# The second mixer of a two-block transformer on one core, put in another order: stick breaking by pairs of heads, output products moved up, values projected as features

## Chip, cores and metric

One NeuronCore of one Trainium2 chip runs the whole program in one launch. The metric is device time in microseconds, the median of three runs.

## What is computed

The input is 256 tokens of width 1024. A first block (two layers of half-step gated feed-forward, attention and gated feed-forward) comes before the part that is changed and is the same in both kernels. The second block begins with the mixer of the reference, cut here to its core:

```
proj = rms_norm(x) @ w_in        # q_a 512, k_a 128, v_a 128, q_b 512, k_b 512, v_b 512, gates 2 x 1024
y_a  = window attention with sinks (8 query heads, 2 key heads of 64), q and k normed per head
y_b  = stick breaking (8 heads): z = q k / 8; log_keep = log_sigmoid(-z) before the diagonal, else 0
       suffix = reversed cumsum(log_keep) - log_keep
       weights = exp(log_sigmoid(z) + suffix) before the diagonal, else 0;  y_b = weights @ v_b
x = x + (sigmoid(gate_a) * (y_a @ w_up_swa) + sigmoid(gate_b) * (y_b @ w_up_sb)) @ w_out
```

After it comes a feed-forward layer with experts picked by product keys: 16 query units, a choice of 16 rows for each of 8 heads, and 256 gathers of 1 MB (128 rows of two vectors of 1024 numbers).

## The kernel before

**Layout.** Activations stand transposed, as eight tiles of 128 features by 256 tokens. Each matrix is cut into units of 128 x 1024 numbers that stream from HBM into a ring of nine raw buffers. To reach the accuracy of float32, each unit is split in two: ScalarE copies it rounded into `WH` (`hi`, line 639), VectorE subtracts to get `WL` (`lo`, line 969), and each product is three matmuls (lines 535 to 537: high by high, high by low, low by high). WH and WL are rings of five units. A call of `hi` or `lo` for a unit also does the three units after it, as far as the ring is free, and a unit's slot comes free when TensorE has used the unit five places back. A product of one unit with 256 tokens is 24 matmuls of 256 columns.

**Order.** No scheduler orders the work: each engine has its own hand-written program (`pe_program`, `act_program`, `dve_program`, `pool_program`, `sp_program`), runs it strictly in order, and waits on semaphores that count the other engines' steps. A waiting instruction holds up everything behind it on its engine.

**Opening of the mixer.** TensorE makes the four `qa` units and `ka`; VectorE scales each out of PSUM (line 1301). In the pass for `ka` it first multiplies the residual `hT` by the last norm's gains, eight instructions (line 1297), so that this stands ahead of the output of `ka`. ScalarE squares the five results (822), TensorE sums the squares (1877), ScalarE takes roots (824, 826), VectorE reciprocals and the norm (`qk_norm`, 1307 and 1309). `va` is made with tokens as rows: 48 matmuls of 128 columns (1887 to 1889). `vb` is 48 matmuls of 512 columns (1900 to 1902) into banks 2 and 3, and waits for the roots, which are read out of these banks. VectorE scales them (1319, 1327).

**Window attention.** Seven turns of a loop over four pairs of heads (scores, exponent, transposes, values). In each turn a *fill* stands behind the scores: two units of `qb`, `kb` or the gates `gt`, 48 matmuls into bank 7, put out by VectorE (`rest`, line 1343) at the end of its own turn. Fill n waits until the output of fill n-1 is out.

**Stick breaking.** Two halves of four heads, one after the other. Each half: logits (1966, 1967), copy out of PSUM (1381), min(-z, z) (1383), on ScalarE exp (871) and ln(1 + .) (873), two fills, softplus (1386) and two masks, suffix sums by triangular matmuls (1974 to 1976), subtraction (1394), clip (1396), exp (877), two masks (1399, 1400), values (1994, 1995), output split in YH and YL (691, 1035). The first half has one fill more, ahead of its values. With each fill VectorE makes two WL units and then later puts the fill out. In all 5 fills.

**End of the mixer.** ScalarE takes the 16 sigmoids (886). Eight `upab` units follow, each with its left half multiplied with the window branch (YH, YL 0 to 3) and its right half with the stick-breaking branch (4 to 7), 12 matmuls each, through banks 6, 7, 0, 1. VectorE multiplies by the gates (1416), GpSimd adds (609), ScalarE and VectorE split the sum (890, 1408). Then eight `wout` units (192 matmuls, 1025 for their output), which wait for those splits tile by tile, and the query units `pq`.

Of the kernel before, what the change touches and what calls it, by code (L numbers as in the profile page):

```python
# [9 lines left out]
ALU = mybir.AluOpType  # L10
# [4 lines left out]
T = 256  # L15
# [241 lines left out]
def program(nc, wst, cst, x, skt, uv, out, vscr, units):  # L257
    ctx = ExitStack()
    with ctx:
# [95 lines left out]
        Z = flat(AST)[:, 0:1536]  # L355
        W = flat(APT)
        E1 = view(s2, 1536)
        E2 = A[:, used[s2]:used[s2] + 1536]
        assert used[s2] + 1536 <= ARENA
# [66 lines left out]
        s_snk, s_snke = sem("sink_shifted"), sem("sink_exp")  # L426
        s_z, s_zc, s_e1, s_e1l, s_sm, s_cum, s_sbw, s_wm, s_we, s_wk, s_sbp = (sem(n) for n in (
# [198 lines left out]
        def act_program(ac):  # L626
# [196 lines left out]
            ac.wait_ge(s_qas, 1)  # L823
            ac.activation(RS[:, 0:4, :], PS[:, 2:4, :].rearrange("p a (b t) -> p (a b) t", b=2), ACT.Sqrt,
                          bias=c("eps", 1, 2), scale=1.0).then_inc(s_qrs, 1)
            ac.activation(RS[:, 4, :], PS[:, 4, 0:T], ACT.Sqrt, bias=c("eps", 0, 1), scale=1.0 / 64).then_inc(s_qrs, 1)
# [18 lines left out]
            n = 4  # L845
# [23 lines left out]
            for half in range(2):  # L869
                ac.wait_ge(s_e1, half + 1)  # L870
                own(ac.activation(E1, E1, ACT.Exp))
                own.wait()
                ac.activation(E1, E1, ACT.Ln, bias=c("eps", 2, 3)).then_inc(s_e1l, 1)
                fill()
                fill()
                ac.wait_ge(s_wm, half + 1)
                ac.activation(W, W, ACT.Exp).then_inc(s_we, 1)
                if fills[0] < len(FILL):
                    fill()
                for t in (2 * half, 2 * half + 1):  # L880
                    ac.wait_ge(s_sbp, t + 1)
                    copy_out(YH, 4 + t, 6 + t % 2, O_SB + t)
            for t in range(8):
# [74 lines left out]
        def dve_program(dv):  # L958
# [322 lines left out]
            for t in range(5):  # L1281
# [13 lines left out]
                if t == 4:  # L1295
                    for kc in range(8):
                        ins = dv.scalar_tensor_tensor(out=hT[:, kc, :], in0=hT[:, kc, :], scalar=c("gains", 48 + kc, 49 + kc),
                                                      in1=RT[:, 0, :], op0=ALU.mult, op1=ALU.mult)
                    ins.then_inc(s_hf, 1)
# [11 lines left out]

            dv.wait_ge(s_qrs, 2)
            qk_norm(4)
            qk_norm(0)
            lo("va", 0)
            dv.wait_ge(s_used, U("va", 0))
            dv.wait_ge(s_rtk, 2)
            for blk in range(2):
                ins = dv.tensor_scalar(VA[:, blk, :], PS[:, 1, 128 * blk:128 * blk + 128], RTK[:, blk:blk + 1], None, ALU.mult)
            ins.then_inc(s_va, 1)  # L1320
            for t in (1, 2, 3):
                qk_norm(t)
            for t in range(4):
                lo("vb", t)
            dv.wait_ge(s_used, U("vb", 3))
            for blk in range(2):
                ins = dv.tensor_scalar(VB[:, blk, :], PS[:, 2 + blk, :], RTK[:, blk:blk + 1], None, ALU.mult)
            ins.then_inc(s_vb, 1)

            fills = [0]  # L1330

            def fill():
# [6 lines left out]
                lo(name, t + 1)  # L1339

# [32 lines left out]
            def h4(v):  # L1373
                return v.rearrange("p (h k) -> p h k", h=4)

            Zh, Sh, Wh = h4(Z), h4(E2), h4(W)
            mk = c("sbmask").unsqueeze(1).broadcast_to([128, 4, 128])
            for half in range(2):
# [11 lines left out]
                for rest in filled:  # L1390
                    rest()
# [741 lines left out]
```

## Time and profile before

| what | value |
|---|---|
| median of three runs | 2043.84 us (2041.53 to 2045.69) |
| the profiled execution | 2047.32 us, its span 2045.4 us |
| TensorE busy | 1863.1 us, 91% |
| VectorE, ScalarE, GpSimd busy | 1303.7 (64%), 907.0 (44%), 305.9 us (15%) |
| mean granted TensorE clock | 0.969 |
| the mixer's stretch that the diff touches | about 1152 to 1361.5 us of the span |
| gathers of the last layer | from 1379 us to the end, 407 to 410 GB/s |

Of a timeline row the first number is the start and the second the time from there to the end of the row's last instruction; "x4" are four instructions together; in brackets stands how long the engine was idle before it and who released it. Matmuls overlap, so their pitch is read from starts and not from durations. A granted clock of 1.00 is 2.4 GHz and 0.50 is 1.2 GHz.

### The profile page before, as it was taken

Reading aid. Unit: us, or ns where it says so; the run is one execution under the profiler, and the core shown is the slowest. Engines: PE = TensorE matmul, PEld = TensorE weight load, DVE = VectorE, ACT = ScalarE, POOL = GpSimd, SP = SyncE. Lnnn points to the kernel's source line nnn. Section 1 sums busy time; section 2 is a strip of 40 time slices with the busy share of each in tenths; the row PEclk is TensorE's granted clock in tenths of the full one; section 3 lists DMA queues with packets and bytes.
Section 4 is the critical chain, followed back from the end, with each engine's and each line's share of the span. In section 5 each row is a group of like instructions: output and inputs, shape, how many; then the busy total and the mean of one; then the engine's idle time right before and its main releaser. Section 6 shows DMA issues by size and latency. Waiting matters only on the chain.

```text
span 2045.4 us, 29867 instructions
## 1 busy us (share of the span) xinstructions
PE 1863.1 (91%) x11568; PEld 1495.6 (73%) x11568; DVE 1303.7 (64%) x2378; ACT 907.0 (44%) x1865; POOL 305.9 (15%) x340
## 2 busy tenths in 40 slices
PE   7999999999999999999999988899997877778877
PEld 7999889999999999869999878797533322223222
DVE  5555785655655562686555765577587767676454
ACT  4444464444444441474444443543454443444333
POOL 1000101000100010000000100023343333333331
PEclk9999899999999997899999899899999999999999
DMA  7555426955555534205555243249999999999998
GB/s 274 186 186 178 128 77 141 305 186 186 161 186 187 185 114 166 83 22 166 186 186 186 83 144 104 83 165 375 387 422 421 421 422 422 421 421 421 422 421 323
DMA packets 96972, 488.35 MB, mean 239 GB/s; under 512 B 10640, under 2 KB 10896, under 8 KB 63808
## 3 DMA queue, kind: packets, MB, share of 16 engines
q0 software_dynamic: 38368, 274.74, 34.9%
q1 hardware_dynamic: 58464, 211.70, 30.9%
q8 instruction: 92, 1.51, 0.3%
q14 instruction: 48, 0.39, 0.1%
HBM read 482.21 MB, written 4.19 MB: 238 GB/s over the span
## 4 chain that ended last, share of the span: by engine, by line
PE 61%; DMA 12%; DVE 11%; issue 8%; POOL 4%; ACT 3%; another core or an unknown queue 0%; POOLq 0%; ACTq 0%; SPq 0%; DVEq 0%
PE PS L535 16%; PE PS L536 15%; PE PS L537 15%; PE PS L2025 3%; DMA WH<-uv,A 3%; DMA YL<-uv,A 3%; DMA YH<-uv,A 2%; DMA raw<-uv,A 2%; DVE WL L969 2%; PE PS L2046 2%; PE PS L1540 1%; DMA A<-uv,A 1%; DMA WL<-uv,A 1%; DVE XL L977 1%; DMA XF<-uv,A 1%
## 5 line engine op out<-in xcount | busy, mean ns | idle before, releaser
L969 DVE TENSOR_TENSOR WL<-raw,WH 128x1024 fp32r<-128x1024 f32 (+1 forms) x379 | 451.7, 1234 | 92.4 <-ACT WH L639 91.8
L535 PE MATMUL PS<-XH,WH 128*128 128x256 f32 x1632 | 474.1, 290 | 28.9 <-DVE WL L969 15.6
L536 PE MATMUL PS<-XL,WH 128*128 128x256 f32 x1632 | 466.3, 286 | 0.0
L537 PE MATMUL PS<-XH,WL 128*128 128x256 f32 x1632 | 466.2, 286 | 0.0
L639 ACT ACTIVATE WH<-raw 128x1024 fp32r<-128x1024 f32 (+1 forms) x379 | 375.0, 1040 | 68.4 <-PE PS L537 41.4
L535 PEld LDWEIGHTS PS<-XH,WH 128*128 128x128 f32 x1632 | 315.5, 193 | 37.8 <-issue 18.8
L536 PEld LDWEIGHTS PS<-XL,WH 128*128 128x128 f32 x1632 | 316.3, 194 | 0.2
L537 PEld LDWEIGHTS PS<-XH,WL 128*128 128x128 f32 x1632 | 315.7, 193 | 0.0
L912 ACT ACTIVATE A<-A,RTK 128x1 f32<-128x1 f32 x256 | 75.0, 293 | 297.8 <-DVE A L1511 296.2
L535 PE MATMUL PS<-GH,WH 128*128 128x256 f32 x704 | 198.1, 281 | 0.0
L536 PE MATMUL PS<-GL,WH 128*128 128x256 f32 x704 | 197.8, 281 | 0.0
L537 PE MATMUL PS<-GH,WL 128*128 128x256 f32 x704 | 197.8, 281 | 0.0
L680 ACT ACTIVATE A<-A 128x256 f32<-128x256 f32 x88 | 36.8, 418 | 350.7 <-DVE A L998 350.7
L580 POOL TENSOR_TENSOR A<-hT 128x256 f32<-128x256 f32 x64 | 47.1, 757 | 952.5 <-DVE hT L1013 725.8
L535 PE MATMUL PS<-YH,WH 128*128 128x256 f32 x584 | 167.0, 286 | 4.8 <-DVE A L1117 3.1
L536 PE MATMUL PS<-YL,WH 128*128 128x256 f32 x584 | 165.7, 284 | 0.0
L537 PE MATMUL PS<-YH,WL 128*128 128x256 f32 x584 | 165.6, 284 | 0.0
L998 DVE TENSOR_TENSOR A<-PS,RT 128x512 f32<-128x512 f32 x88 | 60.9, 692 | 149.3 <-PE PS L537 148.7
L2025 PE MATMUL PS<-raw,A 128*128 128x512 f32 x260 | 128.3, 619 | 29.8 <-ACT A L920 27.6
L535 PEld LDWEIGHTS PS<-GH,WH 128*128 128x128 f32 x704 | 132.6, 188 | 0.1
L537 PEld LDWEIGHTS PS<-GH,WL 128*128 128x128 f32 x704 | 132.7, 188 | 0.0
L536 PEld LDWEIGHTS PS<-GL,WH 128*128 128x128 f32 x704 | 132.7, 188 | 0.0
(305 smaller groups left out, 3128.8 us busy)
## 6 DMA issues: line engine op xcount, KB each, us to landing
raw<-wst SPq DMA_DIRECT2D x388, 512.0 KB, 4.5
raw<-wst SPq DMA_DIRECT2D x9, 384.0 KB, 3.7
vscr<-A POOLq DMA_DIRECT2D x1, 3072.0 KB, 36.4
A<-vscr POOLq DMA_DIRECT2D x1, 2048.0 KB, 22.3
C<-cst SPq DMA_DIRECT2D x1, 1236.5 KB, 10.8
raw<-uv,A POOLq DMA_INDIRECT x65
hT<-xin SPq DMA_DIRECT2D x2, 512.0 KB, 4.7
A<-vscr POOLq DMA_DIRECT2D x1, 1024.0 KB, 12.0
```

What stands on the lines that cost most here:

```text
L535: pe.matmul(o, wh, xh, start=start, stop=False, skip_group_check=True)
L536: pe.matmul(o, wh, xl, start=False, stop=False, skip_group_check=True)
L537: return pe.matmul(o, wl, xh, start=False, stop=stop, skip_group_check=True)
L580: po.tensor_tensor(SQ[:, kc, :], hT[:, kc, :], hT[:, kc, :], ALU.mult).then_inc(s_sq, 1)
L639: ac.activation(WH[:, m % SPL, 0:w], raw[:, i % RAW, 0:w], ACT.Copy).then_inc(s_hi, 1)
L680: ac.activation(GS[:, b, 0, :], GS[:, b, 0, :], ACT.Silu).then_inc(s_silu, 1)
L912: own(ac.activation(AG[:, blk, s:s + 1], AV[:, blk, s:s + 1], ACT.Gelu, scale=RTK[:, blk:blk + 1]))
L969: dv.tensor_tensor(WL[:, m % SPL, 0:w], raw[:, i % RAW, 0:w], f32(WH[:, m % SPL, 0:w]), ALU.subtract).then_inc(s_lo, 1)
L977: dv.scalar_tensor_tensor(out=NORMED[p][1][:, kc, :], in0=hT[:, kc, :], scalar=g, in1=f32(NORMED[p][0][:, kc, :]), op0=ALU.mult, op1=ALU.s ...
L998: dv.tensor_tensor(GS[:, b], PS[:, b, :].rearrange("p (a t) -> p a t", a=2), RT[:, 1:2, :].broadcast_to([128, 2, T]), ALU.mult).then_inc(s ...
L2025: ins = pe.matmul(PS[:, YB[blk] + q, :], DG[:, g % 4, :], v[:, 512 * q:512 * q + 512], start=False, stop=s == 127, skip_group_check=True)
L2046: ins = pe.matmul(PS[:, bank_q[n], 0:T], R[:, 128 * kc:128 * kc + 128], XF[:, kc, :], start=kc == 0, stop=kc == 7, skip_group_check=True)
```

## The change

1. `va` is one plain unit product (24 matmuls of 256 columns), ahead of the sums of squares; VectorE scales it into `VT`, TensorE transposes it twice between the second and third `vb` unit, VectorE copies it to `VA`.
2. The root of `ka` comes before the others. `vb` goes to banks 5 and 6 and waits for earlier outputs only. VectorE scales `VB` before the norms of the last two query tiles.
3. The eight multiplications of `hT` move to fill 5 (the sixth turn of the window loop), behind its two WL units.
4. Stick breaking goes by pairs of heads, four of them, two in flight, in orders written out for each engine. The five fills stand between them.
5. `upab` has a bank per unit. The left halves of units 0 to 3 come before and behind the values of the last pair, their right halves after. Sigmoids 0 and 1 precede the last pair's output on ScalarE; the others go between the `upab` steps.
6. The first two `wout` units do their first six tiles each, and then the last two each.

The diff, cut to its core:

```diff
@@ act_program
+            ac.activation(RS[:, 4, :], ...Sqrt...).then_inc(s_qrs, 1)
             ac.activation(RS[:, 0:4, :], ...Sqrt...).then_inc(s_qrs, 1)
-            ac.activation(RS[:, 4, :], ...Sqrt...).then_inc(s_qrs, 1)
...
+            def log1p(p):
+                e1 = E1P[:, p % 2]
+                ac.wait_ge(s_e1, p + 1)
+                own(ac.activation(e1, e1, ACT.Exp))
+                own.wait()
+                ac.activation(e1, e1, ACT.Ln, bias=c("eps", 2, 3)).then_inc(s_e1l, 1)
+            def stick(p):
+                ac.wait_ge(s_wm, p + 1)
+                ac.activation(WP[:, p % 2], WP[:, p % 2], ACT.Exp).then_inc(s_we, 1)
+            def sb_out(p):
+                ac.wait_ge(s_sbp, p + 1)
+                copy_out(YH, 4 + p, 6 + p % 2, O_SB + p)
...
+            log1p(0)
+            fill()
+            log1p(1)
+            fill()
+            stick(0)
+            fill()
+            stick(1)
+            sb_out(0)
+            log1p(2)
+            fill()
+            sb_out(1)
+            log1p(3)
+            fill()
+            stick(2)
+            sb_out(2)
+            stick(3)
+            hi("upab", 0)
+            sigmoid(0)
+            sigmoid(1)
+            sb_out(3)
...
             for t in range(8):
                 hi("upab", t)
+                if t >= 2:
+                    sigmoid(t)
@@ dve_program
-                if t == 4:
-                    for kc in range(8):
-                        ins = dv.scalar_tensor_tensor(out=hT[:, kc, :], ...)
-                    ins.then_inc(s_hf, 1)
...
+            dv.wait_ge(s_used, U("va", 0))
+            dv.scalar_tensor_tensor(out=VT, in0=PS[:, 1, 0:T], scalar=1.0, in1=RT[:, 1, :], ...).then_inc(s_vt, 1)
+            dv.wait_ge(s_qrs, 1)
+            qk_norm(4)
+            lo("va", 0)
+            lo("vb", 0)
             dv.wait_ge(s_qrs, 2)
-            qk_norm(4)
             qk_norm(0)
...
+            dv.wait_ge(s_vtr, 1)
+            dv.tensor_copy(VA, PS[:, 1, 0:T]...).then_inc(s_va, 1)
+            qk_norm(1)
+            for t in range(1, 4):
+                lo("vb", t)
+            dv.wait_ge(s_used, U("vb", 3))
...
             ins.then_inc(s_vb, 1)
+            qk_norm(2)
+            qk_norm(3)
... in fill(), behind its two lo():
+                if n == 5:
+                    for kc in range(8):
+                        ins = dv.scalar_tensor_tensor(out=hT[:, kc, :], ...)
+                    ins.then_inc(s_hf, 1)
... logits: copy out, min(-z, z); log_weight: subtract, clip; weight: two masks
+            logits(0)
+            logits(1)
+            rest = fill()
+            softplus(0)
+            rest()
+            rest = fill()
+            log_weight(0)
+            softplus(1)
+            rest()
+            weight(0)
+            rest = fill()
+            log_weight(1)
+            logits(2)
+            sb_low(0)
+            rest()
+            weight(1)
+            rest = fill()
+            logits(3)
+            softplus(2)
+            sb_low(1)
+            rest()
+            rest = fill()
+            log_weight(2)
+            softplus(3)
+            rest()
+            weight(2)
+            log_weight(3)
+            sb_low(2)
+            weight(3)
+            lo("upab", 0)
+            sb_low(3)
@@ pe_program
+        UP_BANK = (5, 0, 1, 4, 6, 7, 2, 3)
+            pe.wait_ge(s_qa, 2)
+            gemm("va", 0, 0, 8, X, PS[:, 1, 0:T]).then_inc(s_used, 1)
             for t in range(5):
                 pe.wait_ge(s_qaq, t + 1)
...
-            pe.wait_ge(s_qrs, 1)
+            pe.wait_ge(s_rtk, 2)
+            pe.wait_ge(s_qa, 3)
...
+            sb_logits(0)
+            sb_logits(1)
+            fill()
+            sb_suffix(0)
+            fill()
+            sb_suffix(1)
+            sb_values(0)
+            sb_logits(2)
+            fill()
+            sb_values(1)
+            sb_logits(3)
+            fill()
+            sb_suffix(2)
+            fill()
+            sb_suffix(3)
+            sb_values(2)
+            for t in range(3):
+                up_swa(t)
+            sb_values(3)
+            up_swa(3)
+            for t in range(4):
+                up_sb(t)
+            for t in range(4, 8):
+                up_swa(t)
+                up_sb(t)
+            W2 = [weights("wout", t) for t in range(2)]
+            pe.wait_ge(s_m2, 6)
+            for k0, k1 in ((0, 6), (6, 8)):
+                for t in range(2):
+                    for kc in range(k0, k1):
...
```

## Rows read from the trace of the kernel before

**Rows 1.** The page, busy time of each engine.

```profile
PE 1863.1 (91%) x11568; PEld 1495.6 (73%) x11568; DVE 1303.7 (64%) x2378; ACT 907.0 (44%) x1865; POOL 305.9 (15%) x340
```

**Rows 2.** Windows by stage: busy of PE, PEld, DVE, ACT, POOL; clock; DMA share, GB/s.

```profile
1152.20:1181.60 29.40, 26.48 (x116) 22.57 (x114) 22.26 (x30) 9.42 (x11) 0.00 (x0) 0.77 0.32 105
1181.60:1242.50 60.90, 53.80 (x418) 49.76 (x418) 36.81 (x76) 24.82 (x61) 0.00 (x0) 0.94 0.40 128
1242.50:1307.70 65.20, 50.13 (x353) 46.03 (x352) 38.79 (x49) 24.87 (x23) 0.00 (x0) 0.86 0.26 87
1307.70:1338.80 31.10, 27.64 (x216) 26.75 (x214) 20.25 (x25) 19.55 (x35) 7.49 (x8) 0.94 0.48 164
1338.80:1361.50 22.70, 22.70 (x171) 22.70 (x172) 16.92 (x21) 10.62 (x15) 6.25 (x7) 0.88 0.51 170
...
1700.00:2045.40 345.40, 269.24 (x544) 96.70 (x544) 209.04 (x467) 143.55 (x417) 119.63 (x127) 0.98 1.02 407
```

**Rows 3.** Windows around two pauses of TensorE, same columns.

```profile
1156.00:1170.00 14.00, 13.62 (x56) 12.96 (x57) 7.79 (x8) 4.75 (x6) 0.00 (x0) 0.52 0.13 43
...
1273.00:1275.00 2.00, 0.64 (x8) 0.51 (x9) 1.91 (x4) 0.00 (x0) 0.00 (x0) 1.00 0.87 293
```

**Rows 4.** Timeline of TensorE in the opening.

```profile
1156.38 1.15 PE L1877 MATMUL PS<-A,C 128*128 128x256 f32 x2 [2.28 <-ACT A L822]
1156.97 0.67 PE L1887 MATMUL PS<-WH,XH 128*128 128x128 f32 x1
...
1171.07 0.40 PE L1901 MATMUL PS<-WL,XH 128*128 128x512 f32 x1
...
1179.70 0.40 PE L1902 MATMUL PS<-WH,XL 128*128 128x512 f32 x1
```

**Rows 5.** Timeline of VectorE in the opening.

```profile
1152.29 3.25 DVE L1297 SCALAR_TENSOR_TENSOR hT<-hT,C,RT 128x256 f32<-128x256 f32 x8
...
1159.08 1.75 DVE L1307 RECIPROCAL A<-A 128x256 f32<-128x256 f32 x1 [3.21 <-ACT A L826]
1160.87 0.48 DVE L1309 SCALAR_TENSOR_TENSOR A<-A,C 128x256 f32<-128x256 f32 x1
...
1181.46 2.35 DVE L969 TENSOR_TENSOR WL<-raw,WH 128x1024 fp32r<-128x1024 f32 x2
```

**Rows 6.** Timeline of VectorE in the sixth turn of the window loop.

```profile
1229.96 2.36 DVE L969 TENSOR_TENSOR WL<-raw,WH 128x1024 fp32r<-128x1024 f32 x2 [2.89 <-ACT WH L639]
...
1234.47 0.69 DVE L1343 SCALAR_TENSOR_TENSOR A<-PS,RT 128x512 f32<-128x512 f32 x1 [0.69 <-PE PS L537]
```

**Rows 7.** Timeline of VectorE in the first half of stick breaking.

```profile
1243.41 1.95 DVE L1381 COPY A<-PS 128x384 f32<-128x384 f32 x4 [0.15 <-PE PS L1967]
1245.40 1.76 DVE L1383 SCALAR_TENSOR_TENSOR A<-A 128x1536 f32<-128x1536 f32 x1
1252.55 4.63 DVE L969 TENSOR_TENSOR WL<-raw,WH 128x1024 fp32r<-128x1024 f32 x4 [5.39 <-ACT WH L639]
...
1267.28 0.96 DVE L1396 TENSOR_SCALAR A<-A 128x1536 f32<-128x1536 f32 x1
```

**Rows 8.** Timeline of ScalarE in the same stretch.

```profile
1248.70 1.28 ACT L873 ACT_TABLE_LOAD   x1
1249.99 1.58 ACT L873 ACTIVATE A<-A,C 128x1536 f32<-128x1536 f32 x1
```

**Rows 9.** Timeline of TensorE, first suffix sums of that half.

```profile
1260.24 1.22 PE L1974 MATMUL PS<-A,C 128*128 128x256 f32 x2 [3.31 <-DVE A L1389]
```

**Rows 10.** Timeline of TensorE, within `wout` and at the first `pq` matmul.

```profile
1349.83 0.28 PE L535 MATMUL PS<-XH,WH 128*128 128x256 f32 x1
...
1361.54 0.28 PE L535 MATMUL PS<-YH,WH 128*128 128x256 f32 x1
```

**Rows 11.** Timeline of VectorE, two successive turns of the `upab` loop.

```profile
1326.70 1.76 DVE L969 TENSOR_TENSOR WL<-raw,WH 128x1024 fp32r<-128x1024 f32 x1
...
1329.32 1.76 DVE L969 TENSOR_TENSOR WL<-raw,WH 128x1024 fp32r<-128x1024 f32 x1
```

More of the change, by code:

```diff
@@ L868, in act_program, with sigmoid @@
                     ac.activation(tmp, tmp, ACT.Exp).then_inc(s_snke, 1)
[L869 to L871 removed]
+            def log1p(p):
+                e1 = E1P[:, p % 2]
+                ac.wait_ge(s_e1, p + 1)
+                own(ac.activation(e1, e1, ACT.Exp))
                 own.wait()
[L873 to L883, printed above, removed]
+                ac.activation(e1, e1, ACT.Ln, bias=c("eps", 2, 3)).then_inc(s_e1l, 1)
[5 more added lines that the diff above has]
+                copy_out(YH, 4 + p, 6 + p % 2, O_SB + p)
+            def sigmoid(t):
                 for n in (t, 8 + t):
@@ new lines, in log_weight, with weight @@
+            def log_weight(p):
+                w = WP[:, p % 2]
+                dv.wait_ge(s_cum, p + 1)
+                if p >= 2:
+                    dv.wait_ge(s_sbp, p - 1)
+                dv.tensor_tensor(w, ZP[:, p % 2], PS[:, 2 * (p % 2):2 * (p % 2) + 2, 0:384], ALU.subtract).then_inc(s_sbw, 1)
+                dv.wait_ge(s_sbw, p + 1)
+                dv.tensor_scalar(w, w, 0.0, None, ALU.min).then_inc(s_wm, 1)
+            def weight(p):
+                w = WP[:, p % 2]
+                dv.wait_ge(s_we, p + 1)
+                dv.tensor_tensor(w[:, :, 0:128], w[:, :, 0:128], mk, ALU.mult)
+                dv.tensor_tensor(w[:, :, 256:384], w[:, :, 256:384], mk, ALU.mult).then_inc(s_wk, 1)
@@ new lines, in sb_suffix @@
+            def sb_suffix(p):
+                b0 = 2 * (p % 2)
+                sp_ = E2P[:, p % 2]
+                pe.wait_ge(s_sm, p + 1)
+                for e in range(2):
+                    pe.matmul(PS[:, b0 + e, 0:256], c("ltri"), sp_[:, e, 0:256], start=True, stop=False, skip_group_check=True)
+                    pe.matmul(PS[:, b0 + e, 128:256], c("ones"), sp_[:, e, 256:384], start=False, stop=True, skip_group_check=True)
+                    ins = pe.matmul(PS[:, b0 + e, 256:384], c("ltri"), sp_[:, e, 256:384], start=True, stop=True,
+                                    skip_group_check=True)
+                ins.then_inc(s_cum, 1)
@@ new lines, in sb_values @@
+            def sb_values(p):
+                w = WP[:, p % 2]
+                if p == 0:
+                    pe.wait_ge(s_ol, O_SWA + 4)
+                elif p == 1:
+                    pe.wait_ge(s_fill, 7)
+                else:
+                    pe.wait_ge(s_ol, O_SB + p - 1)
+                pe.wait_ge(s_wk, p + 1)
+                for e in range(2):
+                    oo = PS[64 * e:64 * e + 64, 6 + p % 2, 0:T]
+                    v = slice(128 * p + 64 * e, 128 * p + 64 * e + 64)
+                    pe.matmul(oo, VB[:, 0, v], w[:, e, 0:256], start=True, stop=False, skip_group_check=True)
+                    ins = pe.matmul(oo[:, 128:256], VB[:, 1, v], w[:, e, 256:384], start=False, stop=True, skip_group_check=True)
+                ins.then_inc(s_sbp, 1)
@@ L2012, in begin @@
+            for t in range(2, 8):
+                if t >= 4:
+                    pe.wait_ge(s_h, H0[6] + t - 3)
+                gemm("wout", t, 0, 8, X, PS[:, (6, 7, 0, 1)[t % 4], 0:T]).then_inc(s_used, 1)
             def begin(blk):
```

175 lines of the change are left out of this document (56 added, 119 removed).

## Prediction, made blind

> **What bounds the kernel now.** I read the page first: TensorE is busy 91% of the span [rows 1], but that is an average. The windows by stage say where it is not [rows 2]. In 1152 to 1361.5, the stretch that the diff touches, TensorE is short of work in the opening (26.5 of 29.4 us, at a granted clock of 0.77), in window attention (53.8 of 60.9), most of all in stick breaking (50.1 of 65.2, at 0.86) and in `upab` (27.6 of 31.1). No other engine is full there either (VectorE 38.8 of 65.2 us), so this is a chain of hand-overs. The clock makes each pause dearer: after a pause of 2.28 us [rows 4] the clock stood at 0.52, near the lower of its two levels, until 1170 [rows 3]; after one of 3.31 us [rows 9] it was low too; after one of 2.0 us at 1272 to 1274 it stayed at 1.00 [rows 3].
>
> What is gained here reaches the end. The gathers of the last stage fill the DMA engines (share 1.02, 407 GB/s) [rows 2], start only after the query units and the first choice of rows, which follow `wout` in order, and take as long wherever they start. Weights stream at 87 to 170 GB/s in the mixer [rows 2], so they have room to come earlier.
>
> **Prices.** A matmul of 256 columns at full clock: 1361.54 less 1349.83 over 99 matmuls, 0.118 us [rows 10]; a unit of 24 is 2.84, a fill of 48 is 5.7 and, with what stands between, I take 5.9. A `vb` matmul of 512 columns: 8.63 us over 37, 0.233 [rows 4], so 48 take 11.2. VectorE: a WL unit 1.15 (4.63 for 4) [rows 7]; a norm 1.75 + 0.48 = 2.23 [rows 5]; copy of one head 0.49, min 1.76 for four heads [rows 7]. By pairs I take half of each (0.93 with the fixed part), softplus with masks 1.7, subtraction and clip 1.5 (the clip is 0.96 for four) [rows 7], masks 0.75. ScalarE: ln 1.58 for four heads, 0.92 for two by the slope between that and shorter ones, exp 0.83, a table load 1.28 [rows 8]. Suffix sums of a pair: 1.7 at full clock, 3.4 at half; logits and values 0.8 each.
>
> **Part by part.**
>
> *Opening, −5.1.* The 3.25 us on `hT` [rows 5] leave the path of the output of `ka`, so its square is ready at 1153.4, not 1156.3. TensorE meanwhile does `va` (2.84) and then all five sums, until 1157.3, without the pause of 2.28. `va` and `vb` took 23 us (1156.97 to about 1180) [rows 4], mostly at half clock; the new order has 2.8 + 11.2 and two transposes of about 0.3 and so ends at 1168.8, 11 us earlier. But VectorE doesn't follow. It waits for `va` and for the first root (to 1157.9), and then has a full queue: norm of `ka` 2.2, two WL 2.3, norm 2.2, VA 0.4, norm 2.2, three WL 3.4, VB 1.4, two norms 4.4. It reaches the loop at 1176.4, against 1181.46 [rows 5]. The gain is 5.1; the other 6 us are a pause of TensorE.
>
> *Window attention, +4.4.* In that pause (some 3.4 us before the third scores and 3.3 after, as fill 1 waits for the output of fill 0) the clock falls. Fill 1 then runs partly at half clock. The pause ahead of `wout` kept the clock low for 5.4 us (0.88 over 22.7 us) [rows 2], half of which is lost; I take +1.0, between 0 and 2.7. `hT` now stands in the sixth turn between the WL units and the last softmax scaling [rows 6]; there VectorE has only 0.69 us idle [rows 6] and TensorE's last transposes wait for it: +2.4, and the clock may fall again, +1.0 (0 to 2.7). The stage starts 5.1 earlier and ends 0.7 earlier.
>
> *Stick breaking, −15.7.* Counted from the end of fill 6, with every engine in its written order. Logits of both pairs to 1.6, fill 7 to 7.5. VectorE is done with both minima at 4.5; ScalarE does exp, table load, ln of pair 0 until 5.8 and two WH until 7.7; VectorE, whose WL units stand ahead of softplus(0), gets through those at 9.1 and softplus at 10.8. TensorE has waited 3.3, as before [rows 9], and runs cold: suffix(0) to 14.2, fill 8 to 21.2 (1.3 lost). From there two pairs in flight help: log weight and softplus(1) are done at 18.5, so suffix(1), values(0), logits(2) follow at once, to 24.5. Fill 9 to 30.4. weight(1) stands behind the output of fill 9, so values(1) waits 1.5, to 32.7; logits(3), fill 10 to 39.4; suffix(2), fill 11 to 47.0; suffix(3) and values(2) to 49.5. `upab` starts there, not at 65.2 [rows 2]. Bounds: TensorE's bare work is 42.8 (five fills 29.5, logits 3.3, sums 6.8, values 3.2); each further wait like the first costs 6 (3.3 and 2.7 cold).
>
> *`upab` and `wout`, −6.7.* Before, 53.8 us [rows 2]: cold at the start, and a pause of 2 and 0.5 with a cold 5 us before `wout`, as VectorE's turns of 2.62 [rows 11] run behind. Now 16 units are 45.4 us, values(3) 0.8. VectorE starts its loop 6.4 us after `upab` begins and goes at 2.62 a turn, so the last split is there at 28.7, when TensorE has just done the first six tiles of `wout` 0 and 1; about 1 us is waited: 47.1.
>
> *ScalarE's table.* The trace reloads it before ln and before the exp behind it; each load is 1.28 and ln starts 0.01 after it [rows 8]. Five loads become nine, 5.1 us more of ScalarE. Only that in log1p(0) is on my path, and it was before; the others lie beside fills. The Trainium skill (ScalarE: Activation LUTs, "What ACT_TABLE_LOAD costs") says a switch costs about 1.38 us of drain besides; by it the gain would be at least 1.4 us less. The same page ("Table sets: the hidden batching unit") has a set that holds exp and ln, with which the count would fall to two; the trace doesn't show that set's use.
>
> *No cost:* root order, banks, the first two `wout` units in two parts: same instructions, with other work beside them. SP's load of the sub-keys and two of the gather targets wait for the last values, which come earlier.
>
> *Sum:* −5.1 + 4.4 − 15.7 − 6.7 = −23.1. I give back 1.6 for some thirty hand-overs at about 0.05 each: −21.5. From 2047.3 of the profiled execution that is 2025.8; it was 3.5 above the median, so 2022.
>
> **Rivals.**
>
> *More waits in stick breaking.* With in-order queues a slip of 1 us makes one of the later hand-overs late, above all weight(1) and softplus(2), which stand behind fill outputs and WL units. Two further waits of 6: 2034. For: VectorE has 41.6 us of work in 51.8, so little slack. Against: my schedule has 1 to 3 us in hand at the other hand-overs. 0.13.
>
> *The clock.* The new pause before fill 1, or the one by `hT`, is followed by as long a low clock as 1156 to 1170 [rows 3], at half speed on work that now counts: up to 7 us, 2029. For: nearly 7 us idle in the first. Against: that stretch had 128-column matmuls that keep TensorE less busy; here dense work follows. 0.09.
>
> *Each table load costs twice its length.* One of the four exp-load-ln chains is on my path; with all four on it, and each later by another 1.28 us [rows 8], it is 1.3 to 5.1 more, 2023 to 2027. The trace speaks against (0.01 us between load and ln). 0.03. This is the drain of the Trainium skill's page (ScalarE: Activation LUTs), named above.
>
> *Slower.* The pairs don't overlap, because each log1p waits behind WH copies and each softplus behind WL units. One pair alone is 19.3 us (copy, min, exp, load, ln, two WH, two WL, softplus, cold sums, subtract and clip, exp, masks, cold values); four are 77, 12 more than 65.2; with −0.7 and −6.7 that is 2048. It decides from 73 us for the stage on, where the gains elsewhere are used up. Against: the second pair's logits and minimum need nothing of the first pair. 0.03.
>
> *It doesn't reach the end.* If the gathers started by something other than the query units, the end would stay near 2042. I find no such wait. 0.02.
>
> The forecast has 0.70. About 0.2% (4 us) is what a measurement of this kernel can tell from no change. Range: the best, with TensorE never waiting in stick breaking (−6.7) and no cold fills (−2), is 2013; the upper end takes in the clock rival and most of the further waits, 2033. Faster 0.94, same 0.02, slower 0.04.
>
> **What would show it.** Right: `va` in some 2.8 us, `vb` at clock 1.00, VectorE at the loop near 1176; a pause of TensorE there; +2.4 at the sixth turn; suffix(0) after a pause of 3 us and no other of over 2 in stick breaking; `upab` from about 1291, `pq` from about 1339, gathers as long as before. Wrong: stick breaking of over 55 us, or a clock under 0.9 in window attention.

## The result, and the profile after

The changed kernel takes 2024.46 us (median of 4 runs, 2020.02 to 2026.44) against 2044.76 for the kernel before in the same session: a ratio of 0.9898, with a 95% interval of 0.988 to 0.9916. That is 20.3 us less. The forecast was 2022, with 2013 to 2033 as its range. The profiled execution of after took 2020.02 us, its span is 2018.2, its mean granted clock 0.975.

The page's first part, of after, answers to [rows 1]. TensorE is busy 15.5 us less with 22 matmuls fewer. About 2.5 of these are `va`, whose 24 matmuls take 2.8 us where 48 of 128 columns take 5.4 at the same clock (u_open below); most of the rest is the clock at which TensorE does the same work:

```profile
PE 1847.6 (92%) x11546; PEld 1482.5 (73%) x11546; DVE 1304.3 (65%) x2384; ACT 913.4 (45%) x1875; POOL 305.1 (15%) x340
```

The windows by stage, of after, answer to [rows 2]. The bounds are events: the mixer's first reciprocal (1144.26), VectorE at the window loop (1179.59), the end of fill 6 (1244.12), the first `upab` matmul (1291.65), the first `pq` matmul (1338.89), the first gather (1356.51). The last line is the stretch of the gathers.

```profile
1144.30:1179.60 35.30, 35.30 (x244) 31.88 (x242) 29.69 (x35) 16.02 (x20) 0.00 (x0) 1.00 0.42 135
1179.60:1244.10 64.50, 50.19 (x361) 45.76 (x360) 39.96 (x85) 23.97 (x60) 0.00 (x0) 0.87 0.35 112
1244.10:1291.60 47.50, 42.33 (x345) 39.83 (x344) 37.20 (x51) 30.11 (x31) 0.00 (x0) 1.00 0.35 114
1291.60:1338.90 47.30, 47.09 (x396) 46.23 (x394) 38.88 (x51) 31.21 (x51) 13.69 (x15) 1.00 0.57 189
1338.90:1356.50 17.60, 17.03 (x133) 16.45 (x132) 12.84 (x42) 9.54 (x19) 0.79 (x1) 1.00 0.28 94
1700.00:2018.00 318.00, 248.45 (x504) 88.71 (x503) 189.06 (x414) 132.68 (x385) 108.91 (x116) 0.98 1.02 406
```

The same four stages cut out of two traces of each kernel (the second of each is from the runs below), beside the forecast, in us. The forecast is the stage of the profiled before plus the term of the prediction.

| stage | before | before again | after | after again | forecast |
|---|---|---|---|---|---|
| opening: first reciprocal to window loop | 40.61 | 38.94 | 35.33 | 35.33 | 35.5 |
| window loop to end of fill 6 | 61.00 | 61.13 | 64.53 | 64.53 | 65.4 |
| stick breaking, to first `upab` | 65.26 | 63.70 | 47.53 | 48.79 | 49.5 |
| `upab`, `wout`, to first `pq` | 53.82 | 52.92 | 47.24 | 47.24 | 47.1 |
| sum | 220.69 | 216.69 | 194.63 | 195.89 | 197.6 |

From the first `pq` matmul to the first gather are 17.62 us in all four. From the first `pq` matmul to the end of the span are 683.9, 681.3, 679.3 and 681.8: what the mixer gains reaches the end. One trace says more than the runs do: first against first gives 26.1, second against second 20.8, the times 20.3. The kernel before differs from itself by 4.0, and the granted clock differs with it (0.83 and 0.87 in the opening, 0.86 and 0.90 in stick breaking).

TensorE's pauses of over 1.5 us in this stretch, timeline of TensorE, of after, less one before fill 3 and one before the products of turn 4 that before has too. They answer to [rows 4] and [rows 9]:

```profile
1183.14 1.66 PE L1991 MATMUL PS<-A 64*128 64x128 f32 x8 [3.46 <-DVE A L1382]
1187.35 0.58 PE L537 MATMUL PS<-XH,WH 128*128 128x256 f32 x1 [2.55 <-DVE A L1373]
1187.73 0.42 PE L538 MATMUL PS<-XL,WH 128*128 128x256 f32 x1
...
1234.35 0.87 PE L1666 MATMUL PS<-C,A 128*128 128x128 f32 x6 [2.25 <-DVE A L1084]
...
1255.24 0.70 PE L2031 MATMUL PS<-A,C 128*128 128x256 f32 x2 [3.57 <-DVE A L1419]
...
1274.11 0.66 PE L2049 MATMUL PS<-A 128*64 128x256 f32 x4 [1.54 <-DVE A L1434]
```

Each is a pause that the prediction names: 3.46 and 2.55 before the third scores and before fill 1 (forecast 3.4 and 3.3), 2.25 at `hT` (2.4), 3.57 before suffix(0) (3.3), 1.54 before values(1) (1.5). The line at 1187.73 and its successor, 0.21 later, show fill 1 at the low clock; at full clock they are 0.118 apart [rows 10].

### The profile page after: what moved, and what is told of

It reads as the page before. It is cut to its first block, busy times and chain, and to the rows that moved or that the text cites. A ratio compares the mean times of both kernels' runs of the same rounds, so it can differ in the third digit from the quotient of the medians.

```text
span 2018.2 us, 29835 instructions
## 1 busy us (share of the span) xinstructions
PE 1847.6 (92%) x11546; PEld 1482.5 (73%) x11546; DVE 1304.3 (65%) x2384; ACT 913.4 (45%) x1875; POOL 305.1 (15%) x340
## 4 chain that ended last, share of the span: by engine, by line
PE 62%; DMA 13%; issue 9%; DVE 8%; POOL 5%; ACT 3%; POOLq 0%; ACTq 0%; SPq 0%; DVEq 0%
PE PS L537 17%; PE PS L538 16%; PE PS L539 16%; PE PS L2117 3%; DMA A<-uv,A 3%; DMA WH<-uv,A 2%; PE PS L2138 2%; DMA XF<-uv,A 2%; DMA raw<-uv,A 2%; DMA WL<-uv,A 2%; PE PS L1606 1%; POOL raw L624 1%; DVE WL L995 1%; DMA YL<-uv,A 1%; DVE XL L1003 1%
```

## The experiments

Each compares with the kernel before on the same chip. Two traces of one kernel differ by 1 to 4 us in the mixer, and most intervals below are 0.3% wide; so a part is judged by its stage in the trace, and the time says only whether the stage's gain reached the end.

### The two kernels once more

No edit. First the kernel after:

> The changed kernel once more, as the anchor of this set. Theory (the mixer's stretch is 26 us shorter by the two traces, and all of it reaches the end): 22 to 26 us faster than the kernel before, more than the 20.3 of the first medians. Rival (part of it is lost behind the mixer, where the gathers begin): 20 again, with the stretch from the first pq matmul to the end longer than the 683.9 us of before. In its trace the pause of some 3.5 us ahead of the first suffix sums is followed by a full clock again (theory: a full clock there is chance and may turn out low this time).

2023.97 us, ratio 0.9901 (0.9884 to 0.9918), 21.3 us less in the medians: neither the 22 to 26 of the theory nor the rival's loss behind the mixer, for the stretch from the first `pq` matmul on is 681.8 and not over 683.9. And the kernel before against itself:

> The kernel before once more, for a second trace. In the traces of the changed kernel and its four variants the mixer begins (first reciprocal of VectorE) at 1141.5 to 1148.0 us, in the one trace of before at 1140.85; the stretch from there to the first pq matmul is 25 to 26 us shorter after the change, the timed gain 20 to 21. Theory (the part ahead of the mixer drifts by a few us from run to run, whatever the kernel): here the mixer begins at 1141 to 1148 too, and the stretch to pq takes 220.7 us again to within 1.5. Rival (the change costs some us ahead of the mixer): it begins at 1140 to 1141 again.

2044.79 us, ratio 0.9999 (0.9988 to 1.0011): some 0.1% is what such a comparison can't tell. The mixer begins at 1143.83, as the theory had it, but the stretch to `pq` is 216.7 and not 220.7 to within 1.5. Windows by stage of the kernel before, this second time:

```profile
1143.83:1182.77 38.94, 36.17 (x210) 32.19 (x208) 32.74 (x43) 15.15 (x20) 0.00 (x0) 0.87 0.32 101
1182.77:1243.90 61.13, 53.88 (x417) 49.84 (x417) 36.96 (x77) 24.95 (x61) 0.00 (x0) 0.94 0.39 127
1243.90:1307.60 63.70, 48.61 (x354) 44.74 (x353) 38.79 (x49) 24.86 (x23) 0.00 (x0) 0.90 0.26 90
1307.60:1360.52 52.92, 48.40 (x387) 47.61 (x386) 37.17 (x46) 30.18 (x49) 13.71 (x15) 0.96 0.50 170
```

The instructions and the busy times of VectorE (38.79 in stick breaking) are those of the first trace; the clock is not. The second trace of after has the same pause of 3.58 before suffix(0) as the first has of 3.57, and the sums behind it run at half speed. Timeline of TensorE, after again:

```profile
1256.46 1.22 PE L2031 MATMUL PS<-A,C 128*128 128x256 f32 x2 [3.58 <-DVE A L1419]
1257.47 0.63 PE L2032 MATMUL PS<-A,C 128*128 128x128 f32 x2
```

### One pair after the other (u_serial)

```diff
@@ act_program
-            log1p(0)
-            fill()
-            log1p(1)
...
+            for p in range(4):
+                log1p(p)
+                fill()
+                stick(p)
+                if p == 0:
+                    fill()
+                if p < 3:
+                    sb_out(p)
```

VectorE's and TensorE's orders are changed alike.

> Stick breaking by pairs, but one pair after the other on every engine, with one fill in each and two in the first; all else as changed. Theory (two in flight is what pays): one pair alone is a chain of 16.5 to 19.5 us, so the stage becomes 68 to 74 us for 47.5, the kernel 20 to 25 us slower than the changed one and about level with before. Rival (the smaller pieces pay, the overlap adds little): 3 to 8 us slower than the changed one.

2052.12 us, 1.0034 (1.0021 to 1.0046): slower than before by 0.3%. Stick breaking takes 75.9 us, against 48.8 in after again, and the rest is as in after: `upab` to `pq` 47.22. The forecast was 68 to 74 us for the stage, and 20 to 25 us over after for the kernel, where 28 were measured. Timeline of TensorE, the pauses of the first two pairs:

```profile
1261.33 1.22 PE L2007 MATMUL PS<-A,C 128*128 128x256 f32 x2 [4.32 <-DVE A L1411]
...
1283.48 1.22 PE L2007 MATMUL PS<-A,C 128*128 128x256 f32 x2 [4.33 <-DVE A L1411]
1290.66 1.13 PE L2025 MATMUL PS<-A 128*64 128x256 f32 x4 [3.40 <-DVE A L1426]
```

Then follow 3.64, 3.40 and 2.85. Two in flight are worth 27 us; cutting the heads into pairs without it costs 11 to 12 against the halves of before (65.3 and 63.7), and values(3) isn't even in the 75.9, as three left halves of `upab` stand ahead of it here too. So stick breaking gains by the overlap, and not by the smaller pieces; what the left halves add is measured next.

### The old `upab` and `wout` (u_end)

```diff
@@ pe_program
-            for t in range(3):
-                up_swa(t)
             sb_values(3)
-            up_swa(3)
-            for t in range(4):
-                up_sb(t)
...
+            for t in range(8):
+                b = (6, 7, 0, 1)[t % 4]
...
+                gemm("upab", t, 0, 4, Y, PS[:, b, 0:T], ...)
+                gemm("upab", t, 512, 4, Y, PS[:, b, T:2 * T], ...).then_inc(s_used, 1)
+            project("wout", (6, 7, 0, 1) * 2, X, (s_ml, 0), ...)
@@ act_program
-            hi("upab", 0)
-            sigmoid(0)
-            sigmoid(1)
             sb_out(3)
+            for t in range(8):
+                sigmoid(t)
```

> The end as before: all values, all 16 sigmoids, then upab through four banks, then wout unit by unit. Theory: 6 to 8 us slower than the changed kernel (53.8 us for 47.2 of upab and wout, a little more as the sixteen sigmoids stand behind the last output). Rival (VectorE's turns of 2.6 us set the pace in both, so the banks and the order change little): 0 to 2 us slower.

2034.17 us, 0.9948 (0.9935 to 0.9961): 10.2 above after again, where 6 to 8 were forecast. Two things come back, timeline of TensorE:

```profile
1294.87 0.66 PE L2045 MATMUL PS<-A 128*64 128x256 f32 x4 [2.59 <-DVE A L1431]
...
1325.38 0.39 PE L537 MATMUL PS<-XH,WH 128*128 128x256 f32 x1 [1.98 <-DVE XL L1469]
```

values(3) waits 2.59, as no left halves stand ahead of it, so `upab` begins 52.5 us after fill 6 and not 48.8; and from there to `pq` it is 54.11 and not 47.24, what before had (53.82, 52.92), with the pause before `wout`. The part is worth 10 us, not the 6.7 of its own term. The other 3.7 show in stick breaking: 2.6 are that wait, and about 1.0 is the work of values(3), which here lies ahead of the first `upab` matmul and in after behind it. The banks, the place of the sigmoids and the split `wout` units went back together, and no run tells them apart.

### The old opening, with `hT` left in fill 5 (u_open)

```diff
@@ pe_program
-            pe.wait_ge(s_qa, 2)
-            gemm("va", 0, 0, 8, X, PS[:, 1, 0:T]).then_inc(s_used, 1)
             for t in range(5):
                 pe.wait_ge(s_qaq, t + 1)
...
+            for blk in range(2):
+                q = slice(128 * blk, 128 * blk + 128)
+                o = PS[:, 1, 128 * blk:128 * blk + 128]
+                for kc in range(8):
...
@@ dve_program
-            dv.scalar_tensor_tensor(out=VT, in0=PS[:, 1, 0:T], ...).then_inc(s_vt, 1)
-            dv.wait_ge(s_qrs, 1)
-            qk_norm(4)
-            lo("va", 0)
-            lo("vb", 0)
             dv.wait_ge(s_qrs, 2)
+            qk_norm(4)
             qk_norm(0)
...
```

> The opening as before (va with tokens as rows, vb in banks 2 and 3 behind the roots, old order of outputs and norms), all else as changed; the hT multiplications stay in fill 5. Theory (VectorE's queue sets when the window loop begins, and moving hT is most of the gain): 1 to 3 us slower than the changed kernel, though TensorE's part becomes some 8 us longer. Rival (va and vb on TensorE bound the opening): 8 to 11 us slower.

2022.08 us, 0.9889 (0.9874 to 0.9905): not slower than after, where the theory had 1 to 3 us and the rival 8 to 11. The loop begins 33.68 us after the first reciprocal, 1.65 sooner than with the new opening. Timeline of VectorE at the first root, u_open, and below it after:

```profile
1156.70 1.75 DVE L1328 RECIPROCAL A<-A 128x256 f32<-128x256 f32 x1 [3.25 <-ACT A L828]
```

```profile
1155.84 0.43 DVE L1322 SCALAR_TENSOR_TENSOR A<-PS,RT 128x256 f32<-128x256 f32 x1
1158.67 0.43 DVE L1334 SCALAR_TENSOR_TENSOR A<-PS,RT 128x256 f32<-128x256 f32 x1 [2.41 <-PE PS L539]
1161.34 1.75 DVE L1328 RECIPROCAL A<-A 128x256 f32<-128x256 f32 x1 [2.24 <-ACT A L826]
...
1229.91 3.25 DVE L1367 SCALAR_TENSOR_TENSOR hT<-hT,C,RT 128x256 f32<-128x256 f32 x8
```

From the first reciprocal (1141.45 and 1144.26) that is 15.25 against 17.08. In after VectorE waits 2.41 for `va` and then 2.24 for the root, whose sums stand behind `va` on TensorE.

The old form of `va` is the dearer one on TensorE all the same. Timeline of TensorE, u_open, the first and the last of its 48 matmuls of 128 columns, at clock 1.00:

```profile
1154.80 0.41 PE L1949 MATMUL PS<-WH,XH 128*128 128x128 f32 x1
...
1160.18 0.28 PE L1951 MATMUL PS<-WH,XL 128*128 128x128 f32 x1
```

That is 5.38 us, some 0.11 a matmul, where one of 256 columns takes 0.118 [rows 10]. But from the root to the loop VectorE has no pause in u_open, so its queue and not TensorE sets the loop's start. The edit takes back the order of the roots, the banks and the order of the norms as well; their shares weren't measured.

### `hT` back in the pass over the outputs (u_ht)

```diff
@@ dve_program
+                if t == 4:
+                    for kc in range(8):
+                        ins = dv.scalar_tensor_tensor(out=hT[:, kc, :], ...)
+                    ins.then_inc(s_hf, 1)
...
-                if n == 5:
-                    for kc in range(8):
-                        ins = dv.scalar_tensor_tensor(out=hT[:, kc, :], ...)
-                    ins.then_inc(s_hf, 1)
```

> The changed kernel with the eight hT multiplications back in the pass for ka, all else as changed. The prediction's account (their 3.25 us left the path of the opening and came back as 2.4 in the window loop): the loop begins 3 us later, the loop itself is 2.3 to 3.4 shorter, the kernel within 1 us of the changed one. Rival (in the new order VectorE waits 2.4 us for va right behind the output of ka, so the multiplications would cost 1.0 to 1.6 there): 1 to 2.5 us faster than the changed kernel.

2019.47 us, 0.9883 (0.9868 to 0.9899), an interval that overlaps that of after (0.9884 to 0.9918). The loop begins 35.32 us after the first reciprocal, as in after (35.33): not 3 later, as the theory had it, and not 1.0 to 1.6, as the rival had. Timeline of VectorE:

```profile
1154.85 3.25 DVE L1323 SCALAR_TENSOR_TENSOR hT<-hT,C,RT 128x256 f32<-128x256 f32 x8
1158.02 0.41 DVE L1327 SCALAR_TENSOR_TENSOR A<-PS,RT 128x256 f32<-128x256 f32 x1
1158.35 0.41 DVE L1339 SCALAR_TENSOR_TENSOR A<-PS,RT 128x256 f32<-128x256 f32 x1
1160.48 1.75 DVE L1333 RECIPROCAL A<-A 128x256 f32<-128x256 f32 x1 [1.72 <-ACT A L826]
```

The 3.25 us fill the wait for `va`. With `va` put first `hT` has nothing to gain by leaving. And at the sixth turn it costs: from the first matmul of fill 5 to that of fill 6 are 8.09 us here and in before, 10.90 in after and 11.67 in after again.

### `hT` in the sixth turn, but ahead of its WL units (i_ht)

```diff
-                lo(name, t)
-                lo(name, t + 1)
                 if n == 5:
                     for kc in range(8):
                         ins = dv.scalar_tensor_tensor(out=hT[:, kc, :], ...)
                     ins.then_inc(s_hf, 1)
+                lo(name, t)
+                lo(name, t + 1)
```

> The changed kernel with the eight hT multiplications of fill 5 ahead of its two WL units and not behind them, where VectorE waits 2.9 us for ScalarE. Theory (they make the last transposes of window attention wait 2.25 us and can cost a low clock after it): 2 to 4 us faster than the changed kernel. Rival (the wait is caused by something else that is late too): no change.

2022.65 us, 0.9889 (0.9871 to 0.9908): the time doesn't tell it from after, and the traces have to. `hT` goes into the 2.9 us in which VectorE waits there for ScalarE [rows 6]; the pause of 2.25 is gone and fill 5 to fill 6 is 8.10. Where `hT` stands behind the WL units and the clock falls it is 11.62 (i_soft below), so the place is worth 3.5, of which 2.25 are the wait and the rest the slow transposes behind it; the whole window stage is 63.41 here and 66.91 in i_soft.

### Norms 2 and 3 in the loop's first two turns (i_norm)

```diff
-            qk_norm(2)
-            qk_norm(3)
...
+                if j < 2:
+                    qk_norm(2 + j)
```

The new place is behind the bias of turn j of the window loop.

> The changed kernel with the norms of the last two query tiles taken out of VectorE's queue ahead of the window loop and put into its first two turns, where it waits 1.9 us for ScalarE's exponents. Theory (VectorE's queue sets the start of the loop, TensorE stands still for 3.5 and 2.6 us because of it and falls to the low clock): 4 to 7 us faster than the changed kernel, with scores 2 no longer late. Rival (the exponents and the outputs of the fills set the pace of the loop, and a norm in a turn makes the turn longer by its 2.2 us): 0 to 1 us faster.

2018.93 us, 0.9873 (0.9852 to 0.9895). The loop begins 30.97 us after the first reciprocal, 4.4 sooner; the two pauses of 3.46 and 2.55 become one of 2.83; of the 4.4 us the window stage gives 0.8 back (65.37). The difference of the ratios is 0.0028, 5.7 us, within the 4 to 7 of the theory, but the two intervals overlap.

### The same, and `va` wide but behind the sums (i_open)

```diff
@@ pe_program
-            gemm("va", 0, 0, 8, X, PS[:, 1, 0:T]).then_inc(s_used, 1)
...
+            gemm("va", 0, 0, 8, X, PS[:, 1, 0:T]).then_inc(s_used, 1)
@@ dve_program
+            dv.wait_ge(s_qrs, 1)
+            qk_norm(4)
             dv.wait_ge(s_used, U("va", 0))
             dv.scalar_tensor_tensor(out=VT, ...)
-            dv.wait_ge(s_qrs, 1)
-            qk_norm(4)
```

> The changed kernel with va, still as one wide unit, behind the sums of squares and not ahead of them, and the last two norms in the window loop's first turns. Theory (va ahead of the sums delays the roots by its 2.8 us, and that is why the old opening was no slower): the roots come 1.8 us or more earlier after the mixer's begin, the loop begins 27.5 to 29.5 us after it (35.3 in the changed kernel), the kernel is 5 to 8 us faster than the changed one. Rival (TensorE's vb units bound it from here): the loop begins at 31, as with the norms alone moved.

2015.98 us, 0.9868 (0.985 to 0.9886). Loop at 29.63, TensorE's largest pause at its begin 1.49, fill 1 at full clock in 5.66 (first to last matmul) where after has 7.70. So the place of `va` ahead of the sums costs 1.3. The wide form spares TensorE 2.5 us; what it is worth for the loop's start isn't shown, as the old form wasn't run with the norms in the loop.

### The next softplus ahead of the fill's WL units (i_soft, i_soft2)

```diff
@@ i_soft, dve_program
             logits(1)
-            rest = fill()
             softplus(0)
+            rest = fill()
             rest()
...
-            rest()
             weight(1)
+            rest()
```

```diff
@@ i_soft2, the same and
-            rest = fill()
-            log_weight(0)
             softplus(1)
-            rest()
+            log_weight(0)
+            rest = fill()
             weight(0)
+            rest()
             rest = fill()
             log_weight(1)
```

> The changed kernel with softplus(0) ahead of the two WL units of fill 7 on VectorE, and the masks of pair 1 ahead of the output of fill 9. Theory (the pause of 3.5 us before the first suffix sums and that of 1.5 us before values(1) are VectorE's order alone): 3.5 to 6 us faster than the changed kernel, suffix(0) right behind fill 7. Rival (ScalarE's exp, table load and ln are what softplus waits for): suffix(0) starts no more than 1 us earlier.

> The changed kernel with softplus(0), softplus(1) and log weight 0 all ahead of VectorE's next WL units, and the masks of pair 1 ahead of the output of fill 9. With softplus(0) alone moved, the pause of TensorE went from the first suffix sums to the second (0.4 and 3.3 us), where VectorE waited for WH copies behind ScalarE's second log1p. Theory (softplus(1) can be done at the end of that log1p, so the queue order on VectorE is all that is in the way): no pause over 1.5 us in stick breaking but one before values(0), the stage 44.5 to 46 us long, the kernel 2.5 to 5 faster than the changed one. Rival (ScalarE's chain of two log1p with their four table loads and four WH copies bounds it whatever VectorE does): a pause of 2 to 3.5 stays and the stage takes 47 to 49.

i_soft: 2023.68 us, 0.9895 (0.9879 to 0.9912), stick breaking 48.6: no gain that the time can tell, where 3.5 to 6 were expected. The pause before suffix(0) is gone, and the same pause stands before suffix(1). Timeline of TensorE and of VectorE, i_soft:

```profile
1251.08 0.70 PE L2031 MATMUL PS<-A,C 128*128 128x256 f32 x2 [0.36 <-DVE A L1419]
1262.07 1.22 PE L2031 MATMUL PS<-A,C 128*128 128x256 f32 x2 [3.29 <-DVE A L1419]
```

```profile
1249.27 0.96 DVE L1416 SCALAR_TENSOR_TENSOR A<-A 128x768 f32<-128x768 f32 x1 [1.30 <-ACT A L876]
...
1256.53 2.36 DVE L995 TENSOR_TENSOR WL<-raw,WH 128x1024 fp32r<-128x1024 f32 x2 [2.63 <-ACT WH L641]
1258.81 0.95 DVE L1426 TENSOR_TENSOR A<-A,PS 128x768 f32<-128x768 f32 x1
...
1260.27 0.95 DVE L1416 SCALAR_TENSOR_TENSOR A<-A 128x768 f32<-128x768 f32 x1
```

VectorE is early, and then waits 2.63 for the WH copies that stand behind log1p(1) on ScalarE, with softplus(1) queued behind them. i_soft2 takes softplus(1) and log weight 0 past those too, and puts the masks of pair 0 ahead of fill 8's output: 2017.84 us, 0.9884 (0.9868 to 0.9899), stick breaking 45.49, the largest pause 1.34. Timeline of TensorE, i_soft2:

```profile
1251.48 0.70 PE L2031 MATMUL PS<-A,C 128*128 128x256 f32 x2 [0.35 <-DVE A L1419]
1262.28 0.66 PE L2049 MATMUL PS<-A 128*64 128x256 f32 x4 [1.34 <-DVE A L1434]
```

### All that helped, together (i_best)

i_open, i_ht and i_soft2 in one kernel.

> All mends together: va behind the sums, last two norms in the loop, hT ahead of the WL units of fill 5, the stick-breaking order of i_soft2. Theory (each mend is worth what it is worth alone): 10 to 14 us faster than the changed kernel, 2010 to 2014. Rival (TensorE is then full and the gains overlap): 6 to 9 us faster.

2010.05 us (2005.82 to 2010.32), 0.9838 (0.9824 to 0.9851): faster than before by 1.6%, and than after by about 0.6%, the intervals well apart. Windows by stage, i_best:

```profile
1141.01:1170.63 29.62, 29.62 (x197) 26.34 (x196) 25.51 (x30) 15.38 (x20) 0.00 (x0) 1.00 0.40 131
1170.63:1232.15 61.52, 52.94 (x409) 49.15 (x409) 43.92 (x89) 24.62 (x61) 0.00 (x0) 0.94 0.39 128
1232.15:1277.62 45.47, 42.63 (x345) 39.89 (x345) 37.04 (x51) 29.95 (x31) 0.00 (x0) 1.00 0.38 126
1277.62:1324.87 47.25, 47.05 (x395) 46.22 (x393) 38.85 (x51) 31.22 (x51) 13.70 (x15) 1.00 0.57 190
```

The sum is 183.86 against 195.89 of after again: 5.7, 3.0 and 3.3 from the first three stages, 12.0 in all, and 0.0063 of 2044, 12.9, by the ratios. In the last stage TensorE has 47.05 busy of 47.25; nothing is left there for a new order.

## Why the prediction was right, point by point

**The opening, −5.1: the size right, the account of it wrong.** The working gives the first root at 17.05 after the first reciprocal and the loop at 35.5; measured 17.08 and 35.33. `vb` ran at clock 1.00, and TensorE's other 6 us are the two pauses, 3.46 + 2.55. Against the two traces of before the gain is 5.3 and 3.6; the forecast was counted from the first, and that it fits so well is in part the low clock of that trace. But the step says that it comes from `hT` leaving the path, with `va` filling TensorE's pause beside it. The runs show that the two edits take one and the same wait: with the old order of `va`, moving `hT` gives 33.68; with the new one and `hT` in place 35.32; with both 35.33. The second isn't free where the first is done: `va` ahead of the sums holds the root back by 1.8. The prediction costed the queue of VectorE in full and took TensorE's pause of 2.28 [rows 4] as free room, without asking how long `va` with its wait is compared with it.

**Window attention, +4.4: measured +3.5 and +3.4.** The wait at `hT` is 2.25 (forecast 2.4). The clock's share was put at 1.0 for fill 1 and 1.0 for the sixth turn. Fill 1 took 7.70 and 6.97 from first to last matmul against 5.66, so 2.0 and 1.3; the sixth turn with its wait 2.8 and 3.6 (forecast 3.4), and fill 6 in one of the two traces 6.84. Fill 3 gave back 1.5: it took 7.18 in before and 5.66 in both of after. Two things were not in the term: the wait of 0.95 that before has ahead of fill 2 is gone, and fill 4 took 6.40 in before, 6.57 in after and 7.69 in after again. In runs where fill 3 was slow as well the same code took 66.9 (i_soft, i_soft2), with fill 1 at 8.0. That is what came of the rival on the clock, 1.5 over the forecast of the stage and not up to 7 over the kernel's. Its "against" isn't borne out: in [rows 3] TensorE is busy 13.62 of 14.00 us with the 128-column matmuls, and in u_open the same matmuls ran at clock 1.00. I had written that a clock under 0.9 here would show the prediction wrong. It was 0.87 and the stage came out within 0.9: the granted clock is a mean over the pauses too, and at 1181 to 1191, where it was 0.53, TensorE did 5.3 us of work in 10. Low clock in a pause costs nothing. The sign was badly chosen; the busy time at either pitch is what had to be looked at.

Windows of after ahead of the first pauses, around them and around suffix(0), to set beside [rows 3]:

```profile
1137.00:1170.00 33.00, 33.00 (x207) 29.93 (x206) 21.47 (x25) 15.54 (x21) 0.00 (x0) 1.00 0.40 128
1181.00:1191.00 10.00, 5.31 (x25) 4.62 (x26) 7.82 (x15) 3.85 (x11) 0.00 (x0) 0.53 0.46 144
...
1252.30:1256.00 3.70, 0.76 (x4) 0.71 (x5) 3.46 (x6) 3.66 (x4) 0.00 (x0) 1.00 0.55 172
```

**Stick breaking, −15.7: right, a little better.** 48.79 in the trace in which the suffix sums ran at the low clock, as assumed (49.5 forecast), 47.53 in the one where it did not. By steps from the end of fill 6, forecast against after again: suffix(0) at 10.8 and 11.13, fill 8 at 14.2 and 14.50. There fill 8 ran at full clock (5.65), where 1.3 was allowed for, and values(1) began at 31.26 for 31.9. Why suffix(0) is late is as told. Timeline of VectorE, of after, for [rows 7]:

```profile
1251.17 2.36 DVE L995 TENSOR_TENSOR WL<-raw,WH 128x1024 fp32r<-128x1024 f32 x2 [2.25 <-ACT WH L641]
1253.44 0.95 DVE L1416 SCALAR_TENSOR_TENSOR A<-A 128x768 f32<-128x768 f32 x1
```

Softplus has its input at 1250.2 and starts at 1253.44, behind two WL units that wait for WH. i_soft2 shows that this order, not the work, made the pause: without it 45.5, 2.7 above the 42.8 that I had as TensorE's bare work (which counts values(3), though the next stage has it). The 41.6 us of VectorE's work in 51.8 that I gave for the rival with more waits have no working; VectorE was busy 37.20 in 47.50. That rival didn't come: no other pause is over 1.54. The slower rival is u_serial. It was put at 77 us for the stage and 75.9 were measured; so its size was right and its condition, that nothing overlaps, was not met.

**`upab` and `wout`, −6.7: measured −6.6 and −5.7**, 47.24 for 47.1. u_end shows that the part also carries 2.6 of stick breaking's gain, in the left halves that cover the wait of values(3). The prediction booked that under the stage before.

**ScalarE's table: nine loads, and no drain seen.** Timeline of ScalarE, of after, for [rows 8]:

```profile
1247.09 0.85 ACT L874 ACTIVATE A<-A 128x768 f32<-128x768 f32 x1 [7.64 <-DVE A L1411]
1247.95 1.28 ACT L876 ACT_TABLE_LOAD   x1
1249.25 0.94 ACT L876 ACTIVATE A<-A,C 128x768 f32<-128x768 f32 x1
1250.09 1.99 ACT L641 ACTIVATE WH<-raw 128x1024 fp32r<-128x1024 f32 x2
1252.10 1.28 ACT L874 ACT_TABLE_LOAD   x1
1253.39 0.84 ACT L874 ACTIVATE A<-A 128x768 f32<-128x768 f32 x1
...
1261.32 0.85 ACT L880 ACTIVATE A<-A 128x768 f32<-128x768 f32 x1 [1.63 <-DVE A L1428]
```

Nine loads there are, as forecast, from the first logarithm to the first sigmoid. Behind six of them the next instruction starts 0.01 to 0.02 after the load. Behind the other three it starts 1.58 to 1.64 after, when VectorE has made its input, so that these three can't tell. The Trainium skill (ScalarE: Activation LUTs, "What ACT_TABLE_LOAD costs") has about 1.38 us of drain besides; none is seen at the six, among them the one of the first pair that is on the path, and the rival that rested on it falls. The loads aren't free of effect, though: in i_soft the two around exp(1) stand ahead of the WH copies for which VectorE waits 2.63.

**The sum.** −23.1 and 1.6 given back for hand-overs make −21.5; the times say −20.3. The hand-overs were not seen as a term: three of four stages came out 0.2 to 2.0 below their forecast, the fourth 0.1 above. The times agree with the second pair of traces (20.8). The first pair's 26.1 is 5.3 more: 4.0 are the first trace of before, with its lower clock in the opening, in stick breaking and in `upab` and `wout`, and 1.3 the first of after, whose clock stayed up at suffix(0). These executions were 2.6 above and 4.4 below their runs' medians.

What stays open: why a pause of the same length leaves the clock at 1.00 in one run and halves it in another. No run here was made to tell.

## What to carry to other kernels

Before work is put into a pause, look at how long it takes with its own waits, and whether another edit fills the same pause: each may earn alone what both earn together. Splitting a chain into smaller pieces pays only with the next piece in flight; here that was 27 us, and splitting alone cost 11 or more. In an in-order queue a short step on the critical chain goes ahead of bulk copies whose inputs are late, and on every engine of the chain, else the pause moves to the next piece.

## What the runs showed of the hardware

- The clock after a pause is not set by the pause alone. After 3.57 us before suffix(0) it stayed at 1.00 in after (sums 0.22 apart, then fill 8 in 5.65); after 3.58 in after again the sums ran at half speed and fill 8 at full; in u_open, after 3.57, the sums ran at full speed but for the last few, and fill 8 took 6.87. The same pause cost 0, 1.6 and 1.5 us. The Trainium skill (TensorE: Matmul & The Clock Gate, "Part 1: The HAM clock gate") has the activity monitor running free of the program, so that the number of slow matmuls at the start of one and the same kernel differs from run to run. That after and after again differ behind the same pause agrees with it, though this is the middle of a kernel.
- A slow fill after a pause took from 6.4 (before) to 8.0 us (i_ht, i_soft) instead of 5.66, so 0.7 to 2.4 us are what a low clock took from one fill here.
- `va` in 24 matmuls of 256 columns at full clock left the clock at 1.00 from 1137 to 1170 in after, where the 128-column matmuls of before had 0.52 [rows 3]. The columns alone don't make the difference: u_open has the old 128-column `va` without that pause, and its clock in the opening is 1.00 as well. The wide form behind the pause wasn't run.
- A matmul of 128 columns is hardly cheaper than one of 256. At full clock the 48 of `va` follow each other at some 0.11 us (5.38 us from the first to the last, u_open) and those of 256 columns at 0.118 [rows 10]; at the low clock both are 0.21 apart (`va` in before; fill 1 in after, from 1187.73 on).
